# Swapping the exponential of the scores and the weights in ScalarE's order, in the stick-breaking stage of a hybrid decoder step

## What is computed

```python
z = jnp.einsum('bqhd,bkhd->bhqk', q, k) / math.sqrt(HEAD_DIM) + bias
log_1m = jnp.where(mask, jax.nn.log_sigmoid(-z), 0.0)          # mask: k_pos < q_pos
rest = lax.cumsum(log_1m, axis=3, reverse=True) - log_1m
a = jnp.where(mask, jnp.exp(jax.nn.log_sigmoid(z) + rest), 0.0)
return jnp.einsum('bhqk,bkhd->bqhd', a, v)
```

## Time and profile before

| | us |
|---|---|
| median of three runs | 3379.3 |
| lowest and highest of them | 3362.28 and 3381.38 |
| the profiled execution | 3368.72 |
| its span, first to last instruction | 3367.0 |

### The profile page before, as it was taken

The page is one execution under the profiler, slowest core; times in us unless marked ns, Lnnn a source line. Parts: engine busy times, 40 slices in busy tenths (PEclk is TensorE's granted clock), DMA queues, the critical chain, the costliest instruction groups (busy, mean ns, idle before and its releaser), DMA issues. The chain is left out here.

```text
span 3367.0 us, 52913 instructions
## 1 busy us (share of the span) xinstructions
PE 2926.0 (87%) x17550; PEld 2087.6 (62%) x17550; DVE 1638.3 (49%) x2729; ACT 1380.2 (41%) x2618; POOL 676.5 (20%) x1175
## 2 busy tenths in 40 slices
PE   8999889998898999997999938777888866599998
PEld 5888658887555555555788735445455442388887
DVE  2000042322787888886566624333343433666663
ACT  3122142222676766775555513323332322333332
POOL 0000011221334343441000012333333400000000
PEclk9999999999899999999999969998998987799999
DMA  5444444445101010004322249999999967423321
GB/s 180 159 169 164 153 162 155 170 160 178 62 1 38 1 38 1 17 7 114 87 67 57 72 153 352 386 383 386 379 378 385 375 255 266 165 95 114 118 81 40
DMA packets 316166, 548.77 MB, mean 163 GB/s; under 512 B 65650, under 2 KB 159314, under 8 KB 312852
## 3 DMA queue, kind: packets, MB, share of 16 engines
q1 hardware_dynamic: 273428, 344.54, 30.4%
q0 software_dynamic: 42496, 201.23, 16.2%
HBM read 485.95 MB, written 126.68 MB: 182 GB/s over the span
## 5 line engine op out<-in xcount | busy, mean ns | idle before, releaser
L1356 POOL DMA_DIRECT2D sbs_v_ring<-in_cache_v_sb x512 | 276.2, 539 | 887.8 <-issue 886.6
L416 PE MATMUL proj_ps_G<-proj_w_hi,proj_xT_hi 128*128 128x512 f32 x1024 | 401.5, 392 | 4.0 <-DVE proj_xT_lo L288 4.0
L420 PE MATMUL proj_ps_G<-proj_w_hi,proj_xT_lo 128*128 128x512 f32 x1024 | 398.9, 390 | 0.0
L418 PE MATMUL proj_ps_G<-proj_w_lo,proj_xT_hi 128*128 128x512 f32 x1024 | 398.8, 389 | 0.0
L1603 PE MATMUL sbs_ps_T<-sbs_ident,sbs_k_ring 128*128 128x128 f32 x2048 | 290.5, 303 | 103.4 <-DMA sbs_k_ring<-in_cache_k_sb 90.3
L1442 DVE COPY sbs_kT<-sbs_ps_T 128x512 f32<-128x512 f32 x256 | 176.3, 689 | 415.0 <-PE sbs_ps_T L1603 414.5
L1603 PEld LDWEIGHTS sbs_ps_T<-sbs_ident,sbs_k_ring 128*128 128x128 f32 x2048 | 259.0, 157 | 145.4 <-DMA sbs_k_ring<-in_cache_k_sb 99.6
L360 ACT ACTIVATE proj_out<-proj_ps_G,proj_stat 128x512 f32<-128x512 f32 (+1 forms) x136 | 93.2, 688 | 565.9 <-PE proj_ps_G L420 561.1
L288 DVE TENSOR_TENSOR proj_xT_lo<-proj_ps_T,proj_xT_hi 128x512 fp32r<-128x512 f32 (+1 forms) x68 | 42.2, 663 | 508.2 <-ACT proj_xT_hi L350 508.2
L688 DVE TENSOR_TENSOR sbp_sp_lo<-sbp_sp,sbp_sp_hi 128x512 fp32r<-128x512 f32 (+3 forms) x320 | 243.2, 799 | 59.7 <-POOL sbp_sp_hi L632 57.3
L632 POOL CAST sbp_sp_hi<-sbp_sp 128x512 fp32r<-128x512 f32 (+3 forms) x320 | 198.7, 638 | 253.1 <-DVE sbp_sp L682 249.0
(11 more groups left out here) (280 smaller groups left out, 5766.9 us busy)
## 6 DMA issues: line engine op xcount, KB each, us to landing
sbs_v_ring<-in_cache_v_sb POOLq DMA_DIRECT2D x512, 256.0 KB, 6.0
sbs_k_ring<-in_cache_k_sb SPq DMA_DIRECT2D x512, 256.0 KB, 9.9
out_k_win_s<-in_cache_k_win POOLq DMA_DIRECT2D x16, 2044.0 KB, 8.4
out_v_win_s<-in_cache_v_win POOLq DMA_DIRECT2D x16, 2044.0 KB, 8.1
proj_out<-in_w_in SPq DMA_DIRECT2D x32, 512.0 KB, 5.5
proj_x_in<-in_x_prompt SPq DMA_DIRECT2D x32, 512.0 KB, 3.7
dls_k_in<-in_cache_k_win SPq DMA_DIRECT2D x16, 1024.0 KB, 11.0
dls_v_in<-in_cache_v_win SPq DMA_DIRECT2D x16, 1024.0 KB, 14.7
```

Of the source, the lines that this page charges most:

```text
L416: nc.tensor.matmul(ps_G[0:n, g, :], xT_hi[:, slot, k, 0:n], w_hi[:, k, cols], start=(k == 0), stop=False)
L418: nc.tensor.matmul(ps_G[0:n, g, :], xT_hi[:, slot, k, 0:n], w_lo[:, k, cols], start=False, stop=False)
L420: mm = nc.tensor.matmul(ps_G[0:n, g, :], xT_lo[:, slot, k, 0:n], w_hi[:, k, cols], start=False, stop=(k == KC - 1))
L1356: eng.dma_start(ring[:, q % RING, i, :], cache[bass.ds(page, 1), :, :].rearrange("a s c -> (a s) c")) \
```

## The change

In ScalarE's loop the exponential of the scores of entry k + 2 is issued behind the weights of entry k instead of ahead of them. No instruction is added or removed, no wait changes, and the order of the other engines stays as it is.

```diff
                     fill(x, y)
                 if new == "turn":
                     put_out(x, y)
-                if new == "step":
-                    exp(x)
                 if kind == "step":
                     weights(g)
                 if new == "step":
+                    exp(x)
                     ln(x)
                 if kind == "step" and g + 1 < G and step(g + 1)[3] > 0:
                     left(g + 1)
```

## The result

The changed kernel takes 3386.15 us in the median of 20 executions (3378.76 to 3395.21), the kernel before, measured beside it, 3376.76 (3362.28 to 3381.38). The ratio is 1.0035, with a 95% interval of 1.0027 to 1.0043: 11.8 us slower, 9.1 to 14.5. (The two medians themselves lie 9.4 us apart.) The profiled execution of the changed kernel has a span of 3388.2 us.

What follows compares the result with a forecast made beforehand. TensorE was taken to bound runs of full tiles, the chain VectorE, GpSimd, VectorE the diagonal tiles. Losses 7.2 + 2.8 + 1.5 = 11.5 us on a mean of 3372.9 gave 3384.4, said as 3385, range 3364 to 3403.

Steps and rivals of the forecast that it cites:

- A full step costs nothing: In runs of full tiles: softplus about 0.48 us late, L775 in time by 0.07, the step stays 4.20 us.
- The round that the prediction named, once in three iterations: Totals, sums, weights, exp, ln, softplus, L701, L775, totals: 12.5 us against TensorE's 12.6 in a run of full tiles.
- The ends of runs: Where short diagonal tiles follow full ones, the 0.48 us lateness comes out once: 15 places, 7.2 us.
- The lost overlap: Where softplus waits last for ln, exp directly ahead of ln costs about 0.14 us: 20 places, 2.8 us.
- about 0.1 each: Sign: softplus waits for ln far oftener than 11 times, by 0.1 us each.
- The start: At the stage's first steps an uncovered exp is added, about 0.8 us, then 0.6: together about 1.5 us.
- TensorE's busy time unchanged, 11 us of idle time: Sign: the stage grows from 703 to about 714 us, all TensorE idle time, in its waits for GpSimd.
- A gain of up to 9 us: At TensorE's waits for weights, 6.2 + 2.7 us, earlier weights might gain; taken as 0, chance 0.10.
- TensorE freed: Rival: weights first frees TensorE's loads, up to 92.8 us, time 3280; more gain than 9 us had chance 0.03.
- Adds up: Rival: L775 makes totals 0.48 us late each iteration; 3406 us over 69 iterations, 3436 over 131; chance 0.10.
- Only the overlap on ScalarE's path: Rival: ScalarE bounds, so lost overlap counts in all 131 iterations, 17 us, time 3390; no separate chance given.
- Nothing at all: Rival: other waits cover the ends of runs, only the start's 1.5 us is paid, 3374; nothing to 7 us, 0.22.

Runs made afterwards that it cites:

- e6: The changed kernel with one copy of 128x512 zeros between exp and ln in the 69 iterations whose two tiles are full; stage 719.1 us.
- e4: The changed kernel with six constant matrix products in each of TensorE's six long waits; stage 698.4 us, 1.0012 of the kernel before.
- e5: The kernel before with six constant matrix products in each of TensorE's six long waits; stage 688.5 us, 0.9990 of the kernel before.
- e7: The changed kernel with two copies of 128x512 zeros between exp and ln in the 69 iterations whose two tiles are full; stage 737.0 us.
- e1: The kernel before with the new order only in the 69 iterations whose two tiles are full; stage 699.6 us, 1.0016 of the kernel before.
- e2: The kernel before with the new order only in the 62 iterations holding a diagonal tile; stage 696.8 us, 1.0014 of the kernel before.

## Why the prediction came out as it did

The time, 3386.15, is 1 us from the forecast of 3385, and the sum of 11.5 us stands beside 11.8. That the time is hit to 1 us is luck: the forecast set out from 3372.9, the mean of four executions, and the median of before over twenty is 3376.76, so the same sum on the right base gives 3388.3. What bears on the mechanism is the difference, 11.5 against 11.8 (9.1 to 14.5). By its own steps:

**A full step costs nothing: right; its margin was mis-sized.** The step is 4.20, TensorE 32.83 of 33 us busy, the weights 0.04 behind the sums, softplus to L701 3.45 against a predicted 3.44. L775 ends 0.10 ahead of the load (0.07 predicted). But the load's start is not the limit: e6 has it 0.17 later against its product at almost no cost. The round that the prediction named, once in three iterations, is the one that binds first in e6; its length was 12.33 us and not 12.5, a margin of 0.27 in 12.6 where 0.1 was said. What was off is the first term, 4.6 from the start of the totals' load to the end of the sums: counted from the product itself it is 4.36. (Two small slips beside it: the prediction has softplus 0.48 late, while its own times give 1193.05 - 1192.54 = 0.51, and 20 us on the slowest execution is 3401, not 3403.)

**The ends of runs: right.** At the end of block 1 of the second pair the timeline of VectorE in after reads

```profile
1078.89 1.29 DVE L682 SCALAR_TENSOR_TENSOR sbp_sp<-sbp_Z,sbp_el 128x512 f32<-128x512 f32 x2 [0.41 <-ACT sbp_el L760]
...
1082.34 0.68 DVE L701 TENSOR_TENSOR sbp_LE<-sbp_L,sbp_E 128x512 f32<-128x512 f32 x1
```

Softplus waits 0.41 us for ln where it waited for nothing, and the 3.45 behind it cannot shrink. Fifteen ends at 0.48 and the overlaps make 10.0 us; e4 - e5 has 8.8 for them. Block 1 has 0.45 for an end with its overlaps, the way from pair to pair 0.81; which of the counted ends are partly covered I did not follow up.

**The lost overlap: right in kind and size.** Behind the diagonal tiles of block 3, ScalarE and VectorE of after:

```profile
1154.90 1.02 ACT L767 ACTIVATE sbp_a<-sbp_Z 128x1024 f32<-128x1024 f32 x1
1155.80 1.03 ACT L755 ACTIVATE sbp_el<-sbp_Z 128x1024 f32<-128x1024 f32 x1
1156.86 1.06 ACT L760 ACTIVATE sbp_el<-sbp_el 128x1024 f32<-128x1024 f32 x1
...
1157.95 1.29 DVE L682 SCALAR_TENSOR_TENSOR sbp_sp<-sbp_Z,sbp_el 128x512 f32<-128x512 f32 x2 [0.24 <-ACT sbp_el L760]
```

Weights and exp start 0.90 apart, exp and ln, where the second needs the first, 1.06. The 0.16 is the overlap that the weights between them used to save. The Trainium skill (ScalarE: Activation LUTs, What ACT_TABLE_LOAD costs) gives 93 ns for instructions back to back; 0.10 to 0.12 us is what the rows shown here have, and only for instructions that do not need each other. Softplus waits for ln in 34 places in place of 11: of the 9.9 us more, 1.75 stand at the first step (below), and the other 8.2 come to about 0.35 for each of the 23 new places, so "about 0.1 each" described the lost overlap but not the ends, where the wait shows too.

**The start: right.** ScalarE and VectorE of after:

```profile
853.27 0.38 ACT L767 ACTIVATE sbp_a<-sbp_Z 128x256 f32<-128x256 f32 x1 [4.87 <-PE sbp_Z L836]
853.55 0.81 ACT L755 ACTIVATE sbp_el<-sbp_Z 128x768 f32<-128x768 f32 x1
854.39 0.84 ACT L760 ACTIVATE sbp_el<-sbp_el 128x768 f32<-128x768 f32 x1
...
855.26 1.02 DVE L682 SCALAR_TENSOR_TENSOR sbp_sp<-sbp_Z,sbp_el 128x384 f32<-128x384 f32 x2 [3.51 <-ACT sbp_el L760]
```

From the weights to softplus it is 1.99 us against 1.14 in the earlier trace rows, 0.85 more, the exp that was predicted at 0.8. With the rest of block 0 it came to 0.6, 1.4 and 1.1 us in the three comparisons, of the 1.5 predicted; the clock is low in these first steps, for different lengths, in every one of them.

**TensorE's busy time unchanged, 11 us of idle time: wrong.** Busy time in the stage grew by 7.5 us and idle time by 7.6; between e4 and e5, with the clock held up behind the six waits, by 4.8 and 3.9 (cuts 2.2 us behind the last weights). The step that failed took lateness for idle time. A product that is up to a few tenths late still touches the one before it in the record, as the totals of e6 do (0.51 apart instead of 0.46), and the loss reads as busy. The wait for GpSimd took 5.0 us of the idle time, and the totals' wait for L775 5.1 (10.9 before); the latter the prediction did not name outside full runs.

**The clock: missing from the sum.** No term stood for TensorE's low clock. It adds 2.0 to 3.4 us to the 9.9 of the order. That the total still fits is partly chance: the terms of the order were 1.6 us too high in the sum, the clock's was zero.

**A gain of up to 9 us: taken as 0, rightly.** TensorE's waits for weights fell, from 6.2 and 2.7 us to 3.8 and nothing (and 1.8 at the transposes of the filling), but none of it shows in the stage's length, and the sums' wait for GpSimd and the totals' for L775 grew by more than that. The fall of 6.9 us stayed below the 9 that were named as a sign of error.

**The rivals.** "TensorE freed" is out: the loader's wait for the weights is 71.7 us in after, 21.1 less, and the kernel is slower, so that wait was not TensorE's. The loader did not even wait less there: its idle time ahead of that load that the profile puts to no releaser grew from 11.4 to 35.0 us, and the two together from 104.2 to 106.7. "Adds up" is out by the step of 4.20. "Only the overlap on ScalarE's path" would lengthen the full steps by 0.13, and they are the same. "Nothing at all" is out by the interval, 9.1 to 14.5 us.

## What to carry to other kernels

In this software-pipelined loop a late instruction costs nothing in the stretches where another engine is full, as long as the round it belongs to keeps a margin (in the changed kernel 0.27 us in three steps are left; the further 0.37 of e6 and 0.89 of e7 went beyond it), and about its whole lateness once each time the work changes shape: count the ends of the stretches, not the iterations. Putting the instruction that waits longest ahead of one that is ready won nothing here, and delayed what stood behind it by the work that the ready one had done in the wait. Waits of the weight loader are not waits of TensorE, and a busy share that grows can be lateness as well as work.

## What the hardware showed that I had not expected

- TensorE's clock fell to the lower of its two levels (1.2 of 2.4 GHz) behind a wait of 1.8 to 1.9 us. It fell after the wait had ended, 0.2 to 2.0 us later and with TensorE at work again, and was back some 3 us on. It did so behind all six waits in two executions each of before and after, but only behind four of them in e1 and three in e2, at waits of the same length. The totals products took 1.05 us in it against 0.63.
- Six constant products of 128x512 in the wait, 1.67 us, kept it at 1.00 in all six places. They cost no time of the path and shortened the stage by 5.9 to 6.5 us in before, 8.5 to 9.2 in after.
- The same kernel took 29.6 and 31.3 us for its six steps behind such waits in two executions; elsewhere the two agreed to 0.2 us a step or better, but for the first three steps, where the clock is low as well. Where the low clock falls is the main noise within this stage.
- A weight load that starts 0.17 us later against its product (0.06 ahead of it, not 0.23) moved that product by nothing.
